# Feeding the first two expert blocks of a routed layer from on-chip tokens by selection products, and letting the third expert's matrix load earlier

## The reference

```python
x = layer_norm(ALPHA * x + mix, ln1_g, ln1_b)                  # x1, 544 x 1024
# hier_moe: top-1 of 4 expert groups, then top-2 of the 8 experts in that group, gate = p_group * p_expert
gu = xb @ w_e_in[e];  gt, up = split(gu, 2)                    # 1024 -> 2 x 512
y_block = (silu(gt) * up) @ w_e_out[e]                         # 512 -> 1024
y = sum over the two experts of gate * y_block[token]
x = layer_norm(ALPHA * x + y, ln2_g, ln2_b)
```

## Time and profile before

| | us |
|---|---|
| median of three executions | 1574.96 |
| lowest, highest | 1574.39, 1578.31 |
| the profiled execution, device time | 1575.28 |
| its span, first to last instruction | 1573.2 |

### The profile page before, as it was taken

One profiled execution on the slowest core, in us unless ns is written; L12 is line 12 of the kernel. 1 busy time (PEld: TensorE's weight loads), 2 busy tenths in 40 slices (PEclk: granted clock), 3 DMA queues, 4 the chain that ended last, 5 costly groups with the idle time before them and its releaser, 6 DMA issues.

```text
span 1573.2 us, 34911 instructions
## 1 busy us (share of the span) xinstructions
PE 1466.0 (93%) x14481; PEld 1182.7 (75%) x14481; DVE 697.9 (44%) x1269; ACT 454.9 (29%) x875; POOL 187.4 (12%) x360
## 2 busy tenths in 40 slices
PE   7999999999999999999999999969988887898987
PEld 7999999999988999999988879855544443444442
DVE  5766575676789562223354335574111111111114
ACT  4533535454422452222343333211100000010002
POOL 1110000000000000000000000003432232233323
PEclk9999999999999999999999999979998998999999
DMA  5232435534458322263265462949999999999995
GB/s 206 68 94 80 131 111 166 152 107 142 131 212 300 121 83 93 87 228 91 83 199 205 172 266 76 387 181 377 418 423 423 421 420 421 406 391 420 421 421 229
DMA packets 87683, 368.28 MB, mean 234 GB/s; under 512 B 14584, under 2 KB 37824, under 8 KB 73088
## 3 DMA queue, kind: packets, MB, share of 16 engines
q1 hardware_dynamic: 81408, 357.38, 60.2%
q0 software_dynamic: 6144, 8.95, 1.6%
HBM read 344.82 MB, written 29.31 MB: 238 GB/s over the span
## 4 chain that ended last, share of the span: by engine, by line
PE 74%; DMA 17%; DVE 4%; ACT 2%; issue 1%; SPq 1%; POOLq 0%; POOL 0%; DVEq 0%; ACTq 0%
PE ps L670 36%; DMA arena<-in_w 16%; PE ps L1180 8%; PE ps L814 6%; PE ps L1199 4%; PE ps L920 3%; PE ps L1041 3%; PE ps L901 3%; PE ps L765 1%; PE ps L762 1%; PE ps L954 1%; PE ps L931 1%; PE ps L1164 1%; PE ps L755 1%; DVE cv L1801 1%
## 5 line engine op out<-in xcount | busy, mean ns | idle before, releaser
L1180 PE MATMUL ps<-arena,xT 128*32 128x256 f32 x4096 | 256.9, 403 | 63.4 <-DMA arena<-in_w 62.8
L1180 PEld LDWEIGHTS ps<-arena,xT 128*32 128x32 f32 x4096 | 132.1, 115 | 164.7 <-issue 54.5
L1736 DVE TENSOR_TENSOR wl<-raw,wh 128x1024 fp32r<-128x1024 f32 x151 | 183.4, 1221 | 156.7 <-ACT wh L1271 156.3
L670 PE MATMUL ps<-xh,wh 128*128 128x272 f32 x1136 | 243.3, 295 | 4.1 <-DVE wl L1736 3.0
L670 PE MATMUL ps<-xh,wl 128*128 128x272 f32 x1136 | 235.0, 288 | 0.0
L670 PE MATMUL ps<-xl,wh 128*128 128x272 f32 x1136 | 234.2, 288 | 0.0
L670 PEld LDWEIGHTS ps<-xh,wh 128*128 128x128 f32 x1136 | 179.0, 188 | 15.2 <-issue 9.2
L670 PEld LDWEIGHTS ps<-xl,wh 128*128 128x128 f32 x1136 | 178.4, 188 | 0.0
L670 PEld LDWEIGHTS ps<-xh,wl 128*128 128x128 f32 x1136 | 177.4, 189 | 0.0
L1271 ACT ACTIVATE wh<-raw 128x1024 fp32r<-128x1024 f32 x151 | 158.1, 1055 | 36.6 <-DMA raw<-in_slabs 17.2
L2483 DVE TENSOR_TENSOR hbuf<-sg,ps 128x128 f32<-128x128 f32 x64 | 18.4, 288 | 300.1 <-ACT sg L1588 206.8
(11 more groups left out here) (448 smaller groups left out, 2328.5 us busy)
## 6 DMA issues: line engine op xcount, KB each, us to landing
arena<-in_w SPq DMA_DIRECT2D x96, 2048.0 KB
raw<-in_slabs SPq DMA_DIRECT2D x151, 512.0 KB, 4.4
bc<-acs_dram SPq DMA_DIRECT2D x16, 512.0 KB, 5.9
hs<-in_h SPq DMA_DIRECT2D x16, 512.0 KB, 5.4
out_h_sample<-hs SPq DMA_DIRECT2D x16, 512.0 KB, 4.2
kv<-in_kT SPq DMA_DIRECT2D x8, 1024.0 KB, 4.8
kvx<-in_vc SPq DMA_DIRECT2D x2, 2048.0 KB, 9.8
yld<-ybuf_dram SPq DMA_DIRECT2D x4, 1024.0 KB, 8.5
```

The source lines that it names most:

```text
L670: r = nc.tensor.matmul(ps[:, 2 * (ub % 2) + half, 0:HT], w[:, s, col], x[:, koff + kk, half * HT:half * HT + HT], start=first and kk == 0 ...
L1180: r = nc.tensor.matmul(ps[QS * c:QS * c + QS, 2, 0:2 * FQ], xT[:, s, kk % 2, kk // 2 * QS:kk // 2 * QS + QS], arena[:, at_:at_ + 2 * FQ], ...
L1736: v.tensor_tensor(wl[:, s], raw[:, s], wh[:, s].bitcast(F32), ALU.subtract).then_inc(w_lo, 1)
```

## The change

1. **Selection products.** For blocks 0 and 1 (both of expert 0) the tokens are no longer gathered from HBM. VectorE makes `pick`, a 0/1 tensor that says which token of each tile goes to which of the 64 slots of these blocks, and TensorE multiplies it with x1 on chip: for each block five tiles x four quarters = 20 products of 32 columns (of `pick`) by 256 columns (of x1) into PSUM banks 4 and 5. ScalarE copies each result to `xg`. `turn_x(0)` and `turn_x(1)` wait for these copies (`tr_a`) instead of for gathers. The memsets and gathers for blocks 0 and 1 go; later waits on the gathers' semaphores are counted one lower for these two buffers.
2. **Last tile.** `affine(TT - 1)` is split: `centre` stays, `scale_shift` comes after `pick` and ahead of the rest of `fixed_slots`.
3. **Tables behind the transposes.** `tables(0, ...)` and the first product of the sort stand behind `turn_x(0)`, the second product of the sort behind `gate_up(0)`.
4. **Overflow.** VectorE's `overflow()` moves from ahead of the raising of `h_v` to behind `h_copy(0)`.
5. **Third expert's first matrix.** SP no longer waits for the two gathers ahead of `fetch1(2)`.

```diff
+        pick = place("pick", [P, TT, 2, QS], F32, key2_at)
@@ SP
             store_x1(TT - 1)
-            for s in range(2):
-                sp_.wait_ge(Z[f"g_in{s}"], 16)
             fetch1(2)
@@ TensorE
+            pe.wait_ge(Z["ln_add"], TT - 1)
+            pe.wait_ge(Z["in_v"], 1)
+            for b in range(2):
+                for i, t in enumerate(LN_ORDER):
+                    if i == TT - 1:
+                        pe.wait_ge(Z["ln_add"], TT)
+                    n = min(P, T - t * P)
+                    for c in range(NQ):
+                        r = nc.tensor.matmul(ps[QS * c:QS * c + QS, 4 + b, 0:QD], pick[0:n, t, b], x1[0:n, t, c * QD:c * QD + QD],
+                                             start=i == 0, stop=i == TT - 1)
+                r.then_inc(Z["tr_mm"], 1)
...
-                    pe.wait_ge(Z["in_v"], 2 * phase + k + 1)
+                    pe.wait_ge(Z["in_v"], 2 * phase + k + 2)
...
-            tables(0, ps[:, 7, 0:NBF], inblk_f)
-            pe.wait_ge(Z["srt_v"], 1)
-            nc.tensor.matmul(ps[:, 3, 0:NE], ones[0:NE], cmpT[0:NE], start=True, stop=True).then_inc(Z["srt_mm"], 1)
-            pe.wait_ge(Z["srt_v"], 2)
-            nc.tensor.matmul(ps[:, 7, P:P + 2 * NE], ones[0:NE], onehot[0:NE].rearrange("p a e -> p (a e)"), start=True, stop=True
-                             ).then_inc(Z["srt_mm"], 1)
...
-                pe.wait_ge(Z[f"g_in{s}"], fill if fill is not None else 16 * (n_ // 4 + 1))
+                if fill is None and n_ < 2:
+                    pe.wait_ge(Z["tr_a"], 2 * TT + 1 + n_)
+                else:
+                    pe.wait_ge(Z[f"g_in{s}"], fill if fill is not None else 16 * (n_ // 4 + s // 2))
...
             turn_x(0, 0)
+            tables(0, ps[:, 7, 0:NBF], inblk_f)
+            pe.wait_ge(Z["srt_v"], 1)
+            nc.tensor.matmul(ps[:, 3, 0:NE], ones[0:NE], cmpT[0:NE], start=True, stop=True).then_inc(Z["srt_mm"], 1)
             gate_up(0, 0)
+            pe.wait_ge(Z["srt_v"], 2)
+            nc.tensor.matmul(ps[:, 7, P:P + 2 * NE], ones[0:NE], onehot[0:NE].rearrange("p a e -> p (a e)"), start=True, stop=True
+                             ).then_inc(Z["srt_mm"], 1)
             turn_x(1, 1)
@@ ScalarE
+            for b in range(2):
+                act.wait_ge(Z["tr_mm"], 2 * TT + 1 + b)
+                nc.scalar.activation(xg[b][:], ps[:, 4 + b, 0:QD], ACT.Copy).then_inc(Z["tr_a"], 1)
@@ GpSimd
-            for x_ in xg:
+            for x_ in xg[2:]:
                 p_.done(nc.gpsimd.memset(x_[:], 0.0))
...
-            for n_ in range(4):
+            for n_ in range(2, 4):
                 gather_go(n_, None)
@@ VectorE
-            affine(TT - 1)
+            centre(TT - 1)
...
+                do(v.scalar_tensor_tensor(gkm[:], slot_f[:, :, 0], float(QS * NBF + 1), Msel[:, :, 0], ALU.add, ALU.mult))
+                v.tensor_tensor(pick[:].rearrange("p t b j -> p t (b j)"), gkm[:].unsqueeze(2).to_broadcast([P, TT, 2 * QS]),
+                                riota[:, 0, 1:2 * QS + 1].unsqueeze(1).to_broadcast([P, TT, 2 * QS]), ALU.is_equal
+                                ).then_inc(Z["in_v"], 1)
+                scale_shift(TT - 1)
...
             schedule()
-            overflow()
-
             for n_ in ("h_v", "hT_v", "y_v"):
                 dve.sem_inc(Z[n_], 1)
...
             hidden(0)
             h_copy(0)
+            overflow()
             slots()
             hidden(1)
```

More of the change, by code:

```diff
@@ L1229, in _ @@
                 with pe.Fori(0, NBLK - NB0) as ob:
-                    turn_x(NB0, 1, ob, 1, ix(16 * (NB0 // 4 + 1), ob, 16))
+                    turn_x(NB0, 1, ob, 1, ix(16 * (NB0 // 4), ob, 16))
                     gate_up(NB0, 1, ob)
@@ L2286, in do, with centre @@
                 c_.sync()
-            def affine(i):
+            def centre(i):
                 t = LN_ORDER[i]
@@ L2293, in affine, with scale_shift @@
                 c_.done(v.scalar_tensor_tensor(x1[0:n, t], x1[0:n, t], lmv[0:n, t, 0:1], ln1_row[0][0:n], ALU.subtract, ALU.mult))
+            def scale_shift(i):
+                t = LN_ORDER[i]
+                n = min(P, T - t * P)
                 c_.sync()
                 v.scalar_tensor_tensor(x1[0:n, t], x1[0:n, t], lrs[0:n, t:t + 1], ln1_row[1][0:n], ALU.mult, ALU.add).then_inc(Z["ln_add"], 1)
+            def affine(i):
+                centre(i)
+                scale_shift(i)
             def bc3(ap, n_):
```

## The result

| | changed kernel | kernel before, beside it |
|---|---|---|
| median of 22 executions each | 1578.70 | 1575.87 |
| lowest, highest | 1575.53, 1582.96 | 1574.39, 1578.71 |
| ratio of the two, 95% interval | 1.0013 (1.0007 to 1.0019) | |
| the profiled execution, device time | 1575.53 | 1575.28 |
| its span | 1573.3 | 1573.2 |

The ratio says 2.0 us slower (1.1 to 3.0): less than 0.3%, but on the wrong side of zero, where 2.3 us faster was forecast; the median lies outside the range. (The ratio is estimated from all executions; the two medians by themselves lie 2.8 us apart. So there are two things to explain: why the profile shows no gain, and why the median shows a loss.

What follows compares the result with a forecast made beforehand. The full DMA stream of expert matrices, starting when `gate_up(1)` is done, sets the end. 0.3 + 2.5 - 0.3 = 2.5, taken as 2.3 off 1575.28, gives 1573.0 profiled, 1572.7 us median; range 1569.5 to 1576.5.

Steps and rivals of the forecast that it cites:

- The end of the kernel is the end of `gate_up(1)` plus a constant: Stream of expert matrices: its start follows the end of `gate_up(1)`, forecast at 1072.4 against 1074.80, 2.4 us earlier.
- rival A: Block chain leads the stream: queue runs dry at the issue of 1088.0, only 1.2 us gained, 1573.8; chance 0.12.
- VectorE and SP: Last tile: `pick` out at 1052.95, last store 1.3 later, `fetch1(2)` at about 1054.6, 9.0 earlier than before.
- The picks: 80 selection products on TensorE from 1053.0: clock rises after 4.3 us, done after 6.7 at 1059.7.
- From the picks' end to `gate_up(0)`: Transposes 0.44, table products 1.3, VectorE 2.0: `gate_up(0)` starts at about 1063.7 against 1064.03, buying 0.3.
- I take the clock as kept: TensorE's 1.9 us wait ahead of `gate_up(0)` keeps the high clock: 3.66 for 6.12, a gain of 2.5.
- between the two `gate_up`s: Gap from `gate_up(0)` to `gate_up(1)`: 1.3 us instead of 1.0, the sort's second product now standing there.
- rival C: Picks don't lift the clock, or the gap before `gate_up(0)` loses it: 1578.8 to 1580.0; only gap, 1575.0; chance 0.06.
- The overflow: VectorE, behind `h_copy(0)`: 2.9 us ahead of the slots, `turn_h(1)` waits 1.1 us; nothing taken off the middle.

Runs made afterwards that it cites:

- e6: Kernel before plus filler products nobody reads in TensorE's idle time (seven ahead of the ranks, three of the tables, two of `turn_x(0)`): 1577.43 us, ratio 1.0000.
- e8: Changed kernel with seven filler products ahead of the ranks, semaphores raised before the schedule, and full rows in the last tile's picks: 1571.12 us, ratio 0.9961.
- e10: Changed kernel with semaphores raised before the schedule and full rows in the last tile's picks, without fillers: 1571.61 us, ratio 0.9971.
- e7: Changed kernel with seven filler products ahead of the ranks: 1574.93 us, ratio 0.9989.
- e5: Changed kernel with the last, short tile's selection products taking all 128 rows instead of 32: 1576.49 us, ratio 0.9998.
- e9: Changed kernel with SP holding `fetch1(2)` until the gathers of blocks 2 and 3 have landed: 1580.53 us, ratio 1.0027.
- e4: Kernel before with only `overflow()` moved behind `h_copy(0)`: 1576.42 us, ratio 1.0002.
- e12: Changed kernel run a fourth time, no edit: 1577.16 us, ratio 1.0006 to the kernel before.
- e2: Changed kernel with VectorE raising `h_v` and two other semaphores before it works out the schedule: 1574.41 us, ratio 0.9992.

## Why the prediction was wrong, step by step

**The end of the kernel is the end of `gate_up(1)` plus a constant: held, roughly.** The issue for expert 3 follows it by 0.2 again. R is 498.2 to 498.8 in before and in all profiles of the changed kernel, though it reaches 500.4 in others, most of that by the clock of one block near the end (e6). The 4.4 to 4.7 us won in S arrive whole in e8 and e10, which also rules out rival A; the 2.4 of e6 don't.

**VectorE and SP: right.** `pick` starts at 1052.81 and is out at about 1053.3 (forecast 1052.95, with D 0.5 later), and `fetch1(2)` goes out at 1054.89, less that 0.5 at 1054.4 (forecast 1054.6). The DMA engines are nearly idle from 1067, as forecast: the transfer let go 9 us earlier ran its 4 MB beside the picks.

**The picks: 7.4 instead of 6.7.** They start where forecast, from D, and the clock rose 5.1 us after that rather than 4.3 (4.8 to 5.9 in the four profiles): 0.4 of the 0.7. The rest is the rate, taken from `gate_up` with its full rows: all 80 at the low clock took 9.39, forecast 9.1, and all at the high one 5.06 (e7), forecast 4.6. Picks at the low clock to their end had been given a small chance, and two of the six profiles in which short-row picks began at the low clock have it.

**From the picks' end to `gate_up(0)`: 4.0 us, as forecast.** `turn_x(0)` waits 0.23 for ScalarE's copy, which I hadn't counted, and overlaps the table's products, which I hadn't either; VectorE takes 2.06 for 2.0. So `gate_up(0)` starts 0.7 late, all of it from the picks, and from D 0.4 later than before instead of 0.3 sooner. The step had no margin: it exchanged work of one length for work of the same.

**"I take the clock as kept": the step that failed.** It was taken from one row, 32 products at the high clock after 1.88 us of idle. Here a wait of 1.84 was followed by the fall, in all four profiles of the changed kernel, and in e5 and e9 too, and `gate_up(0)` took 5.35 instead of 3.66. That is 1.7 us. Together: 0.7 for the picks and 1.7 here, less 0.1 between the two `gate_up`s (1.2 for 1.3), make S 2.2 to 2.3 longer than forecast, 34.48 for 32.3. The sum is whole.

The row came from a steady run of wide products; ahead of this wait stand ten products of 6 columns and two of 32, in which the profile counts TensorE as busy. The steady runs of the fourteen profiles say how far the row reaches. I counted every wait of TensorE that began at the high clock, from 5 to 470 us behind `gate_up(1)`: of 71 between 1.2 and 1.94 us none was followed by a fall, even where the clock had risen less than 0.7 us ahead of it; of 32 between 1.94 and 2.35 us 26 were. So behind wide products a wait of 1.84 us kept the clock every time, though it lies close to those that lost it. What is different here is the work ahead of the wait; that this is the reason is likely and not shown, for no run changes it alone. e7 and e10 show both ways out. In e10 the wait is 0.33, and the clock stays; in e7 the wait is 1.84, and it stays, with the clock up since before the picks.

The Trainium skill (TensorE: Matmul & The Clock Gate, HAM oscillation) warns of idle gaps between bursts of products, but of longer ones than this; the trace shows that a shorter one can be enough. The prediction's own rival C, "if only the gap loses it", gave 1575.0, and the profiled execution took 1575.53. That it comes so near is in part luck: C lets the gap take back all of the 2.5 us, where it took 1.7, and leaves out the 0.7 of the picks.

**The overflow: right in kind.** `turn_h(1)` waits 0.51, forecast 1.1, because TensorE came later than forecast. e4 shows 0.75 and no cost.

**The median's 2 us.** In four profiles the changed kernel is within 0.3 us of before up to `gate_up(1)`. What its median has beyond that comes from long executions: 21 of its 51 are above 1578, against 17 of 115 of the kernel before (13 of 22 against 2 of 22 in the first session, 8 of 29 against 15 of 93 later). Among the executions below that line the medians are 1576.4 (30) and 1576.1 (98), as near as the profiles say. The clock's falls in the first 30 us and near the end (e12, e6) add about 1.5 us each; they were seen in kernels with and without the change. A start of the picks at the low clock throughout would give such executions: it adds 2 us, it was seen in two profiles of kernels whose code is the same up to there, and e2's one profiled long execution is of that kind. It was not seen in a profile of the changed kernel itself, whose one profiled long execution, e12's, was long for another reason. So it is a likely cause, not a shown one. That full rows prevent it (no picks at the low clock throughout in the profiles of e5, e8 and e10, and no long execution in 13 of e8 and e10) is likewise open: e5 alone had two of ten above 1578.

## What to carry to other kernels

Replacing a transfer by products moves the wait onto an engine whose speed depends on what it did just before. Count such an edit at the low clock first, and take the high one only where the engine has neither an idle stretch nor a row of narrow products ahead of the work that matters; here letting the next products start without waiting for the schedule, with full rows in the picks (e10), turned a loss of 0.1% into a gain of 0.3%. A row that shows the clock kept over a gap is evidence for that gap with that work ahead of it, not for its length. And two kernels whose waits differ by tenths of a microsecond can differ by 1.5 us far from the change, where such a wait costs the clock; before a gain of that size is called won or lost, look where the profiles part. And a load that is let go earlier should be tried alone and in company: edit 5 costs 3.5 us beside gathers and is worth 3 without them.

## What the runs showed of the hardware

- 80 products of 32 columns by 256 without a break took 9.39 us wholly at 1.2 GHz in two profiles; in four others, with the same instructions up to there, the clock rose after 4.8 to 5.9 us.
- Behind products of 6 and 32 columns the clock fell within 1.0 us of the end of a 1.84 us wait in six profiles, and stayed up in one with fillers ahead (e7). Behind wide products it stayed up over all 71 waits of 1.2 to 1.94 us, and fell behind 26 of 32 of 1.94 to 2.35 us.
- Sixteen of the recorded products took 2.0 us at the low clock where half of them multiply 32 rows, 1.7 us where all multiply 128 (e5).
- A gather of 32 rows took 6.9 us from issue to use beside a load of 4 MB, 3.0 with the queues empty.
- The same code reaches the mark D between 1040.1 and 1043.5 us. In the three latest, 1.5 us of it is one fall of the clock at 24.3 to 24.8 us.
